# A decoder layer on one core: the sample's convolution between its projections, one selection and one load moved forward

## The reference, cut to what matters

```python
z = split_proj(rms_norm(x, g_pre) @ w_in)
q, k, q_idx, k_idx = rope(q), rope(k), rope(q_idx), rope(k_idx)
s = sum_h w_idx[h] * relu(q_idx[h] @ k_idx.T)       # -inf where not valid
_, sel = lax.top_k(s, 256)                          # then attention over the selected
u = z["c_conv"] * z["u"]
conv = z["b_conv"] * short_conv([state, u], conv_w) # times silu(g_conv)
y = x + rms_norm(concat(att, conv, mem) @ w_out, g_post)
```

## Time and profile before

| | us |
|---|---|
| median of three runs | 2413.73 |
| lowest, highest run | 2400.1, 2415.58 |
| the profiled execution | 2410.6 |
| its span in the trace | 2408.8 |
| TensorE, VectorE, ScalarE busy in the span | 2116.4 (88%), 1404.0 (58%), 1200.8 (50%) |
| mean granted clock of TensorE | 0.900 |

### The profile page before, as it was taken

How to read it: one execution, slowest core, us unless ns; L and a number is a source line. 1 busy time by engine, 2 the same in 40 slices (tenths; PEclk the granted TensorE clock), 3 DMA queues, 4 the chain that set the end, 5 groups by cost and what they waited for, 6 DMA issues and landing times. The chain is left out here.

```text
span 2408.8 us, 33367 instructions
## 1 busy us (share of the span) xinstructions
PE 2116.4 (88%) x12592; PEld 1698.6 (71%) x12592; DVE 1404.0 (58%) x3150; ACT 1200.8 (50%) x2337; POOL 113.5 (5%) x174
## 2 busy tenths in 40 slices
PE   7999999989996889889999878999989989979765
PEld 4776676767765767666778658786777868759662
DVE  2334775676643565657866755697576352625680
ACT  1102467777741346466666765566656675422000
POOL 0000000000000000000000000000000000010004
PEclk9999999999996789989999997999988898977556
DMA  7213121221114212120211010110110001032001
GB/s 277 78 52 104 61 75 63 71 69 61 47 48 154 98 48 66 54 67 12 73 59 57 20 58 33 38 53 8 54 42 20 27 21 45 29 135 85 1 4 33
DMA packets 61888, 144.57 MB, mean 60 GB/s; under 512 B 14288, under 2 KB 28536, under 8 KB 60704
## 3 DMA queue, kind: packets, MB, share of 16 engines
q1 hardware_dynamic: 59552, 131.95, 16.5%
q0 software_dynamic: 2176, 10.49, 1.3%
HBM read 100.18 MB, written 42.24 MB: 59 GB/s over the span
## 5 line engine op out<-in xcount | busy, mean ns | idle before, releaser
L1576 PE MATMUL psum<-sb_v,sb_ptb 128*128 128x64 f32 x2176 | 323.0, 296 | 35.3 <-ACT sb_ptb L1179 34.5
L1576 PEld LDWEIGHTS psum<-sb_v,sb_ptb 128*128 128x128 f32 x2176 | 309.5, 218 | 48.8 <-ACT sb_ptb L1179 48.1
L817 PE MATMUL psum<-sb_w,sb_xt 128*128 128x512 f32 (+5 forms) x1088 | 333.9, 463 | 0.5 <-DVE sb_xt L550 0.5
L1179 ACT ACTIVATE sb_ptb<-psum 128x512 f32<-128x512 f32 (+3 forms) x352 | 183.2, 536 | 225.3 <-PE psum L1568 221.2
L817 PEld LDWEIGHTS psum<-sb_w,sb_xt 128*128 128x128 f32 (+1 forms) x1088 | 180.8, 187 | 125.5 <-issue 113.2
L1568 PE MATMUL psum<-sb_con,sb_p 128*128 128x128 f32 x1280 | 222.6, 298 | 49.7 <-ACT sb_p L1198 36.2
L1351 DVE CUSTOM_DVE_ANT_0 sb_p<-psum,sb_bias 128x1024 f32<-128x1024 f32 (+7 forms) x128 | 126.7, 990 | 203.0 <-PE psum L1558 162.7
L856 PE MATMUL psum<-sb_xt,sb_w 128*128 128x128 f32 x2048 | 237.3, 276 | 0.0
L856 PEld LDWEIGHTS psum<-sb_xt,sb_w 128*128 128x128 f32 x2048 | 234.3, 192 | 1.1
L1600 PE MATMUL psum<-sb_wo,sb_mix 128*128 128x512 f32 x512 | 231.9, 596 | 0.0
L295 ACT ACTIVATE sb_lowj<-sb_sc,sb_l_ncand,sb_l_scl 128x1152 bf16<-128x1152 f32 (+7 forms) x128 | 219.7, 1717 | 4.1 <-DVE sb_l_step L256 2.1
(11 more groups left out here) (408 smaller groups left out, 2953.6 us busy)
## 6 DMA issues: line engine op xcount, KB each, us to landing
qt_s<-sb_qt SPq DMA_DIRECT2D x32, 512.0 KB, 2.9
sb_x<-in_x_prompt SPq DMA_DIRECT2D x16, 512.0 KB, 4.6
xt_s<-sb_xt SPq DMA_DIRECT2D x16, 512.0 KB, 2.6
sb_qa<-qt_s SPq DMA_DIRECT2D x16, 512.0 KB, 4.4
sb_qa<-qt_s SPq DMA_DIRECT2D x32, 256.0 KB, 5.8
sb_xres<-in_x_prompt SPq DMA_DIRECT2D x16, 512.0 KB, 4.4
out_y_prompt<-sb_y SPq DMA_DIRECT2D x16, 512.0 KB, 3.0
sb_p<-xt_s SPq DMA_DIRECT2D x9, 512.0 KB, 5.7
```

Source lines behind the costliest of these rows:

```text
L817: mm = pe.matmul(out, m.xt[:, p, k, 0:n], m.w1[:, k, lo:hi], start=(k == 0), stop=(k == KD - 1))
L1179: act.activation(m.ptb[:, g, 0:cols], m.turn[slot][:, 0:cols], ACT.Copy).then_inc(s.t_act, 1)
L1576: mm = pe.matmul(o, m.ptb[:, g, x * P:(x + 1) * P], v, start=st, stop=sp)
```

## The change

It does three things. In `a_vector` the selection of tile 7 moves from the end to the place ahead of the sample's rotations. In `a_tensor` the 64 products of the sample's convolution are no longer issued behind its four projections but between their slices: four behind each of the last four slices of the first projection, two behind each slice of the second, one behind each of the third, three behind each of the fourth. In `a_sync` and `b_sync` the first load of `qi` moves from behind the meeting to the end of the last projection tile, where it waits for the last indexer product of stage A. So that this load overwrites only the buffer that those products read, `qi` gets an address of its own choice in stage B, and `y` and `qa` other ones.

```diff
@@ a_sync
     for i in range(NT):
         tile(i, i % 2)
+    sp.wait_ge(s.e_score, e_first(EARLY))
+    load_both(sp, m.qi, io.qt_s[1, EARLY], s.qi_ld)
...
@@ a_vector
     for i in range(NT):
         tile(i, i % 2)
+    select(NT)
...
     ch.link(dve.tensor_tensor(cvs, cvs, e16, ALU.mult))
-    select(NT)
@@ a_tensor
+    conv = [(bank, cols[j // 2] + (j % 2) * P, j, k) for bank, cols in ((0, (U0, C0)), (1, (B0, G0)))
+            for j in range(4) for k in range(KD)]
+
+    def project_sample(out, lo, hi, done, behind):
+
+        p = SEQ_S % 2
+        for k in range(KD):
+            mm = pe.matmul(out, m.xt[:, p, k, 0:DB], m.w1[:, k, lo:hi], start=(k == 0), stop=(k == KD - 1))
+            if k == KD - 1 and done:
+                mm.then_inc(s.z_done, 1)
+            for _ in range(behind(k)):
+                bank, at, j, kc = conv.pop(0)
+                if j == 0 and kc == 0:
+                    pe.wait_ge(s.zc_read, 2 * NT - 1 + bank)
+                mm = pe.matmul(m.pc[bank][:, j * DB:(j + 1) * DB], m.w1[:, kc, at:at + P], m.xt[:, p, kc, 0:DB],
+                               start=(kc == 0), stop=(kc == KD - 1))
+                if j == 3 and kc == KD - 1:
+                    mm.then_inc(s.zc_done, 1)
...
-    project(m.pz[0][0:DB, :], p, Q0, K0, DB).then_inc(s.z_done, 1)
-    project(m.pz[1][0:DB, 0:256], p, K0, QI0, DB)
-    project(m.pz[1][0:DB, 256:328], p, KI0, U0, DB).then_inc(s.z_done, 1)
-    project(m.pz[2][0:DB, :], p, QI0, KI0, DB).then_inc(s.z_done, 1)
-    pe.wait_ge(s.zc_read, 2 * NT)
-    for bank, cols in ((0, (U0, C0)), (1, (B0, G0))):
-        for j in range(4):
-            lo = cols[j // 2] + (j % 2) * P
-            for k in range(KD):
-                mm = pe.matmul(m.pc[bank][:, j * DB:(j + 1) * DB], m.w1[:, k, lo:lo + P],
-                               m.xt[:, p, k, 0:DB], start=(k == 0), stop=(k == KD - 1))
-        mm.then_inc(s.zc_done, 1)
+    project_sample(m.pz[0][0:DB, :], Q0, K0, True, lambda k: 4 if k >= 4 else 0)
+    project_sample(m.pz[1][0:DB, 0:256], K0, QI0, False, lambda k: 2)
+    project_sample(m.pz[1][0:DB, 256:328], KI0, U0, True, lambda k: 1)
+    project_sample(m.pz[2][0:DB, :], QI0, KI0, True, lambda k: 3)
@@ b_sync
     def load_qi(t):
-        if t > EARLY:
-            sp.wait_ge(s.d_last, t - EARLY)
+        sp.wait_ge(s.d_last, t - EARLY)
         load_both(sp, m.qi, io.qt_s[1, t], s.qi_ld)
...
-    load_qi(EARLY)
     load_xt2(0)
@@ program
-            m.qi = sb(b, "qi", [P, 2, NIH, P], F32R)
...
+            with ExitStack() as own:
+                sb(own, "pad", [P, 72])
+                m.qi = sb(own, "qi", [P, 2, NIH, P], F32R)
+            sb(b, "hold", [P, 72 + 2048])
+            m.qa = sb(b, "qa", [P, 2, NH, P], F32R)
```

More of the change, by code:

```diff
@@ L897, in a_tensor @@
     pe.wait_ge(s.z_read, 3 * NT)
-    project(m.pz[0][0:DB, :], p, Q0, K0, DB).then_inc(s.z_done, 1)
-    project(m.pz[1][0:DB, 0:256], p, K0, QI0, DB)
-    project(m.pz[1][0:DB, 256:328], p, KI0, U0, DB).then_inc(s.z_done, 1)
-    project(m.pz[2][0:DB, :], p, QI0, KI0, DB).then_inc(s.z_done, 1)
-    pe.wait_ge(s.zc_read, 2 * NT)
-    for bank, cols in ((0, (U0, C0)), (1, (B0, G0))):
-        for j in range(4):
-            lo = cols[j // 2] + (j % 2) * P
-            for k in range(KD):
-                mm = pe.matmul(m.pc[bank][:, j * DB:(j + 1) * DB], m.w1[:, k, lo:lo + P],
-                               m.xt[:, p, k, 0:DB], start=(k == 0), stop=(k == KD - 1))
-        mm.then_inc(s.zc_done, 1)
+    project_sample(m.pz[0][0:DB, :], Q0, K0, True, lambda k: 4 if k >= 4 else 0)
+    project_sample(m.pz[1][0:DB, 0:256], K0, QI0, False, lambda k: 2)
+    project_sample(m.pz[1][0:DB, 256:328], KI0, U0, True, lambda k: 1)
+    project_sample(m.pz[2][0:DB, :], QI0, KI0, True, lambda k: 3)
+    assert not conv
     pe.wait_ge(s.sc_ld, 16)
@@ L2354, in program @@
             m.r.append(m.ptb[:].rearrange("p x n -> p (x n)"))
-            m.qa = sb(b, "qa", [P, 2, NH, P], F32R)
-            xt2 = [m.p[:, 0, 1024:2048].rearrange("p (k n) -> p k n", k=KD), m.qa[:, 0].bitcast(F32)]
-            m.xt2 = lambda j: xt2[j > XT_APART]
             m.gate, m.qm = sb(b, "gate", [P, 2, 768]), sb(b, "qm", [P, 256])
@@ L2361, in program @@
             m.mix = sb(b, "mix", [P, KD, P])
-            m.xres, m.y = sb(b, "xres", [P, D]), sb(b, "y", [P, D])
+            m.xres = sb(b, "xres", [P, D])
+            with ExitStack() as own:
[3 more added lines that the diff above has]
+            m.qa = sb(b, "qa", [P, 2, NH, P], F32R)
+            xt2 = [m.p[:, 0, 1024:2048].rearrange("p (k n) -> p k n", k=KD), m.qa[:, 0].bitcast(F32)]
+            m.xt2 = lambda j: xt2[j > XT_APART]
+            m.y = sb(b, "y", [P, D])
             m.late = search_state(b, "l_", 2, LOW)
```

## The result

| | before | after |
|---|---|---|
| median (range) of 13 runs each, us | 2414.2 (2394.32 to 2420.4) | 2432.83 (2419.02 to 2443.91) |
| profiled execution, us | 2410.6 | 2430.24 |

The ratio is 1.007, 95% interval 1.0046 to 1.0095, so 11 to 23 us are lost. The forecast of 2387, and its range, lie on the other side of no change. The executions profiled of spread and part_again (experiments 3 and 6) were slow ones of their kernels (2419.36 and 2417.65 us), so of them the seam alone is read, and all ratios are of fast runs.

What follows compares the result with a forecast made beforehand. The bound was the seam's path: projections, convolution, selection, bias store, `qi`, products. First gate block 24.4 us earlier, after gate weights take some back: 2410.6 - 24.4 = 2386.2, against the median 2389.3; forecast 2387, range 2375 to 2402.

Steps and rivals of the forecast that it cites:

- What is late next: the sample's stores: Stage seam: last rotation's stores become the end; meeting over at 737.2 in place of 756.30, 19.1 us earlier.
- The convolution between the projections: Sample on TensorE: mixed at full clock with 2.0 us of loads hidden, lasts 30.65 us and ends 10.4 us earlier.
- rival 1: TensorE's sample: clock falls inside the mixed stretch; a fall 5.2 us in gives 2407.3; chance 0.11, of it 0.04 slower.
- far end: TensorE's sample: all mixed work at half clock, first gate block 1.9 us later than before, 2412.5 us.
- no load is hidden: Sample's narrow matmuls: 128 full weight loads, sample ends 2.0 us later, 2388.2 us; a rival given chance 0.12.
- The gate weights: Stage B's start: `xt2` and `w2` loads stay behind the meeting, land 14.2 us after it (13.8 to 16.5), leaving 24.4 gained.
- The selection moved: VectorE, tile 7: the 10.47 us selection starts at 699.06, is covered by the projections, and costs nothing.
- `qi` early: Stage B's first load issued about 701.5: its 6.4 us wait is gone, first product 25.4 us earlier.
- faster by over 1%: Whole kernel: outcome given 0.50, beside within 1% 0.46 and slower by over 1% 0.04.
- two thirds of 0.56 and a third of 0.31: Parts of the 0.50: the forecast's own chance 0.56, and unhidden loads 0.12, later weights 0.12, gain given back later 0.07.

Runs made afterwards that it cites:

- spread: Changed kernel, bias and single elements stored before the rotated rows; narrow products four, one, none, three behind each slice of the four projections; 2400.82 us, ratio 0.9933.
- part_again: part_behind measured once more, beside the two kernels with late `qi`; 2392.07 us, ratio 0.9892 to the kernel before.
- sel_qi: Changed kernel with the convolution behind the four projections as before, so only selection and `qi` load moved; 2400.86 us, ratio 0.9942 to the kernel before.
- conv_only: Kernel before with the mixed convolution alone; selection and `qi` load stay where they were; 2428.56 us, ratio 1.01.
- no_elem: Changed kernel without the two stores of single elements (newest row of the sample's convolution state left out); 2419.51 us, ratio 1.0016 to the kernel before.
- part_behind: Changed kernel, bias and single elements stored first; 32 narrow products behind first projection's slices, two behind each last-projection slice, 16 after; 2395.87 us, ratio 0.992.
- part_old_addr: part_late_qi with the addresses of `qi`, `qa` and `y` of the kernel before; 2401.64 us, ratio 0.9935 to the kernel before.
- part_late_qi: part_behind with `qi` loaded behind the meeting, new addresses kept; 2397.3 us, ratio 0.9918 to the kernel before.

## Why the prediction was wrong, by its steps

1. **"What is late next: the sample's stores": failed, 13.3 us.** It saw that the stores become late, and priced them wrongly: the bias row was given its 2.0 us, and "could queue behind the single elements; that is 1 us at most". The row of 2.0 us was of an empty queue, and neither the 1 us nor the landing of the single elements had a row: the kernel before hid it under convolution and selection, so no wait for it was in its trace. From the elements' issue to SP's first load of stage B it is 16.7 to 17.5 us in after, sel_qi and conv_only; without the elements, or with them 32 us earlier, that wait is gone: no_elem takes 4.5 us for this step, less than the 6.15 forecast. A time of 1 us is that of the elements' issue (1.03), not of their landing.
2. **"The convolution between the projections": failed, 19.2 us**, in two terms. About 12.1 us are the clock, rival 1, which was given 0.11 and came about in the third projection, 19.1 us behind the first narrow product (707.01 to 726.1). Its far end (all at half, 2412.5) did not hold the measured time, since it kept step 1's price of the stores. About 7.1 us are the mix at full clock: no load is hidden, where 2.0 us were taken, and each of 28 groups costs 0.17 us on top. Weight loads of the changed kernel around the first groups (PEld):

```profile
707.01 0.97 PEld L838 LDWEIGHTS psum<-sb_xt,sb_w 128*128 128x128 f32 x8 [0.86 <-issue]
707.99 0.10 PEld L831 LDWEIGHTS psum<-sb_w,sb_xt 128*8 128x8 f32 x2
708.95 0.97 PEld L838 LDWEIGHTS psum<-sb_xt,sb_w 128*128 128x128 f32 x8 [0.86 <-issue]
```

   The load at 708.95 starts where the two wide matmuls that began at 708.00 end (1.02 us), and a group of 0.87 (two wide) and 8 x 0.112 (narrow) takes 1.94 us (707.01 to 708.95). The prompt's hidden loads are loads of 128 columns among matmuls of one shape; the sample alternates 8 and 128 columns, and that row did not bear on it. The Trainium skill's rule ("TensorE: Matmul & The Clock Gate", Part 3, "What overlaps and what doesn't") pointed the right way for this mix, though by it the sample would last 32.65 us and it takes about 37.8 at full clock, and the wrong way for the prompt's tiles (138 loads at no idle time).
3. **"The gate weights": right in kind, 2.1 us short.** They were waited for in three places, 2.1 us in all; the last of these ended 15.8 us after SP's first load (787.72 less 771.96), where 14.2 was taken in a range of 13.8 to 16.5.
4. **"The selection moved": right.** It ran 701.21 to 711.67 beside the projections, at no cost. **"`qi` early": right** that no product waits for it; it is worth 3 to 4 us at the first gate block, and the totals don't resolve it.

The chances failed with the steps: a slower result was allowed only through the clock, because the price of the stores was closed at 1 us. With that price open to 17 us the sum runs from 24 us gained to about 10 gained even at full clock, and with the clock's fall to a loss. The 0.50 for "faster by over 1%" is also a little high by its own parts: two thirds of 0.56 and a third of 0.31 are 0.48.

## What to carry to other kernels

Before work is moved from behind a store, ask what the store's landing was hidden by; a store of single elements like this one belongs 17 us and more ahead of any wait for it, and ahead of it in the queue belongs what is needed soon. Narrow matmuls between wide ones cost a change of shape per group (0.17 us here), so put them in few groups; and they can take the clock from the wide ones, so look at the granted clock of each order that you try. Leave the rest where they cover something. An edit of three parts is best priced with each part alone; here two of them were good, and part_behind keeps all three at 0.992 and 0.989.

## What the runs showed that was not expected

- Two stores of 1024 elements of 4 B each leave the DMA engines within about 2 us but are waited for 15.0 us (after) and 15.1 (sel_qi) behind the last issue, and a 256 KB store issued right behind lands in 15.9 us in place of 2.0. The Trainium skill ("DMA: Bandwidth & Descriptors", "Anatomy of one DMA — SWDGE (gpsimd) path") puts most of the fixed cost of some 2 us, for a DMA that GpSimd issues, into the confirmation of the write, the longest where it goes to HBM. These stores are issued by SP; conv_only agrees on the place, since the wait goes on with no packet in flight, and the 15 us are over seven times that size. Why the landing of single elements takes so long no run shows.
- The end of the full clock is not the same in each execution of one order: 36 narrow matmuls at the end of the sample took 6.22 us in part_behind, 5.84 in part_old_addr and 4.18 in part_late_qi (clock 1.00), which on TensorE have the same order.
